# Layers 0 and 1: recurrent values, attention values and gates made by token in one 400-column product, from two weight chunks cut by input block

## The reference, cut to what matters

```
(au, av, az, bq, bk, bv, bz, cq, ck, cv, co, cz, cg) = _split_proj(xn @ w_in)
v_lat = bv.reshape(B_, S, B_KV_HEADS, HEAD_DIM)       # attention values, 2 x 64 columns
ql, kl, vl = mheads(cq), mheads(ck), mheads(cv)       # recurrent heads, 4 x 64 columns
li_f, lf_f, li_b, lf_b = gates(cg)                    # 16 gate columns
```

## Time and profile before

| | |
|---|---|
| median of 3 runs | 1133.12 us (1132.96 to 1134.46) |
| span of the profiled execution | 1130.7 us (the page gives no other time of it) |
| TensorE busy | 1100.2 us, 97% of the span |
| VectorE, ScalarE busy | 722.0 us (64%), 591.5 us (52%) |
| granted TensorE clock | 0.9 or more of full speed in all 40 slices |
| low parts of weights (L420) | 256 of 1.234 us |
| high parts of weights (L405) | 256 of 1.049 us |
| loads | 167.03 MB, mean 148 GB/s; 363 and 318 GB/s in the first two slices of 28 us |

### The profile page before, as it was taken

How to read it: one execution, slowest core, us unless ns; L and a number is a source line. 1 busy time by engine, 2 the same in 40 slices (tenths; PEclk the granted TensorE clock), 3 DMA queues, 4 the chain that set the end, 5 groups by cost and what they waited for, 6 DMA issues and landing times.

```text
span 1130.7 us, 20229 instructions
## 1 busy us (share of the span) xinstructions
PE 1100.2 (97%) x8280; PEld 969.1 (86%) x8280; DVE 722.0 (64%) x1221; ACT 591.5 (52%) x970; POOL 134.2 (12%) x160
## 2 busy tenths in 40 slices
PE   8999999999999999899999999999998999999998
PEld 6787888766777989689988999999997799999997
DVE  5546567376535667767764676766676666776674
ACT  5332666444334556757464664544474646454454
POOL 0000000054020000423232100000013321000000
PEclk9999999999999999999999999999999999999999
DMA  9822212177421333034333445455442234545551
GB/s 363 318 112 75 75 38 75 40 279 278 150 75 41 147 137 134 2 131 168 140 122 113 150 186 198 177 187 186 178 172 101 97 127 139 200 183 187 190 192 47
DMA packets 24428, 167.03 MB, mean 148 GB/s; under 512 B 2832, under 2 KB 3216, under 8 KB 4752
## 3 DMA queue, kind: packets, MB, share of 16 engines
q1 hardware_dynamic: 24336, 165.74, 39.9%
HBM read 164.68 MB, written 1.05 MB: 147 GB/s over the span
## 4 chain that ended last, share of the span: by engine, by line
PE 86%; DVE 5%; ACT 4%; issue 2%; POOL 1%; DMA 1%; SPq 0%; DVEq 0%; ACTq 0%; POOLq 0%
PE bank L426 24%; PE bank L427 23%; PE bank L428 23%; DVE wlo L420 2%; ACT whi L405 2%; PE bank L1522 2%; PE bank L1388 2%; PE bank L472 1%; DMA PROJ<-in_stream 1%; PE bank L1532 1%; PE bank L1542 1%; PE bank L1415 1%; PE bank L1406 1%; PE bank L2489 1%; PE bank L1263 1%
## 5 line engine op out<-in xcount | busy, mean ns | idle before, releaser
L426 PE MATMUL bank<-OPH,whi 128*128 128x256 f32 (+1 forms) x1716 | 524.1, 305 | 5.5 <-ACT AV L2723 2.2
L427 PE MATMUL bank<-OPL,whi 128*128 128x256 f32 (+1 forms) x1716 | 514.5, 300 | 0.0
L428 PE MATMUL bank<-OPH,wlo 128*128 128x256 f32 (+1 forms) x1716 | 514.5, 300 | 0.0
L420 DVE TENSOR_TENSOR wlo<-raw,whi 128x1024 fp32r<-128x1024 f32 x256 | 305.3, 1234 | 103.9 <-ACT whi L405 103.7
L426 PEld LDWEIGHTS bank<-OPH,whi 128*128 128x128 f32 x1716 | 327.8, 191 | 27.1 <-issue 9.8
L427 PEld LDWEIGHTS bank<-OPL,whi 128*128 128x128 f32 x1716 | 328.0, 191 | 12.1 <-issue 1.7
L428 PEld LDWEIGHTS bank<-OPH,wlo 128*128 128x128 f32 x1716 | 327.9, 191 | 11.0
L405 ACT ACTIVATE whi<-raw 128x1024 fp32r<-128x1024 f32 x256 | 255.6, 1049 | 100.7 <-PE bank L428 99.9
L426 PE MATMUL bank<-whi,OPH 128*128 128x256 f32 (+1 forms) x272 | 89.2, 328 | 0.0
L427 PE MATMUL bank<-wlo,OPH 128*128 128x256 f32 (+1 forms) x272 | 87.2, 321 | 0.0
L428 PE MATMUL bank<-whi,OPL 128*128 128x256 f32 (+1 forms) x272 | 87.1, 320 | 0.0
(11 more groups left out here) (289 smaller groups left out, 1200.5 us busy)
## 6 DMA issues: line engine op xcount, KB each, us to landing
raw<-in_stream SPq DMA_DIRECT2D x147, 1024.0 KB, 4.8
PROJ<-in_stream SPq DMA_DIRECT2D x5, 1024.0 KB, 14.9
X<-in_x_in SPq DMA_DIRECT2D x4, 512.0 KB, 6.5
C<-in_con SPq DMA_DIRECT2D x1, 1477.5 KB, 9.6
out<-PROJ SPq DMA_DIRECT2D x4, 256.0 KB, 2.1
WST<-in_w_s SPq DMA_DIRECT2D x2, 256.0 KB, 5.4
PROJ<-in_last_gain SPq DMA_DIRECT2D x1, 512.0 KB, 5.6
BS<-in_b_s SPq DMA_DIRECT2D x1, 256.0 KB, 5.9
```

Source lines behind the costliest of these rows:

```text
L420: nc.vector.tensor_tensor(c.w[1][:, part], c.raw[:, part], c.w[0][:, part].bitcast(F32), ALU.subtract).then_inc(*raises(c.lo[h]))
L426: nc.tensor.matmul(out, w[0], x[0], start=start, stop=False, skip_group_check=skip)
L427: nc.tensor.matmul(out, w[0], x[1], start=False, stop=False, skip_group_check=skip)
L428: return nc.tensor.matmul(out, w[1], x[0], start=False, stop=stop, skip_group_check=skip)
```

## The change

The attention values, recurrent values and gates of a token tile (256 + 128 + 16 = 400 columns) become one job by token, four jobs per layer; ScalarE empties each with two copies into `VA` and into a new `VG`, whose last 16 columns are the gates. The values product, the gate product and their turns go, as does the own load of the gate weights. Attention keys, these 400 columns and no more (528 in all) stand in two head chunks of 128 x 2112: the first holds input blocks 0 to 3, the second blocks 4 to 7. They come first: the first after pair 1, the second after pair 2, and the recurrent keys' chunk after all pairs. The start fills the four jobs and the keys; the two key products follow as whole jobs, `ck_0` before the gate sums and `ck_1` after. The turn of the recurrent keys moves behind `ck_1`. `rotate_keys` uses pairs of 64-column stationary slices of `ident` and `rot16` in place of `dup` and `duprot`.

```diff
-            if i == 1:
-                early = take(2)
+            if i in (1, 2):
+                early += take(1)
...
+    def heads(w):
+        at = [256 * IN_BLOCK[name] for name in ("bkv", "cv")] + [256 * IN]
+        c = np.concatenate([w[:, at[0]:at[0] + P], w[:, at[1]:at[1] + 256], w[:, at[0] + P:at[0] + 256],
+                            w[:, at[2]:at[2] + 16]], 1)
+        return c.reshape(2, 4, P, HEAD).transpose(0, 2, 1, 3).reshape(2, P, WIDE)
...
-                for j in (ck0, ck1):
+                for j in by_token:
                     first.fill_part(e, j, (0, 1))
                 pairs[2].multiply(e, 0)
-                for j in (ck0, ck1):
+                first.fill_part(e, keys, (0, 1))
+                for j in by_token[0:2]:
                     first.fill_part(e, j, (2, 3))
                 pairs[2].multiply(e, 1)
-                first.fill_part(e, keys, (0, 1))
+                for j in by_token[2:4]:
+                    first.fill_part(e, j, (2, 3))
                 pairs[2].turn(e)
+                pairs[3].multiply(e, 0)
                 first.fill_part(e, keys, (2, 3))
-                pairs[3].multiply(e, 0)
-                first.fill_part(e, values, (0, 1))
+                for j in by_token[0:2]:
+                    first.fill_part(e, j, (4, 5))
                 pairs[3].multiply(e, 1)
-                first.fill_part(e, values, (2, 3))
+                for j in by_token[2:4]:
+                    first.fill_part(e, j, (4, 5))
                 pairs[3].turn(e)
...
                 pairs[1].copy_rows(e, "act")
                 split_hi(e, 1)
                 act_operand(e, 1)
-                split_hi(e, 2)
                 pairs[2].copy_rows(e, "act")
                 act_operand(e, 2)
+                split_hi(e, 2)
...
+            heads = [j for j in jobs if j.head is not None]
+            if heads:
+                heads[-1].frees_head = True
+                heads[-1].head[0].used = ("head_half_used", heads[-1].head[0].i)
+                heads[-1].head[1].used = heads[-1].u.full
...
             def split_next(e, who, j):
+                if j.frees_head:
+                    split_ahead(e, who, j.head[1].s + 1 + SPLIT)
...
+            def evict_tokens(e, u, tt):
+                for point in due(e, ("va_ones_set",)):
+                    e.wait_ge(*point)
+                nc.scalar.activation(VA[:, tt, :, 0:HD], u.mem[:, 0:256].rearrange("p (h d) -> p h d", d=HD),
+                                     ACT.Copy).then_inc(*raises(("cv_copied", l, tt)))
+                nc.scalar.activation(VG[:, tt, :], u.mem[:, 256:BY_TOKEN], ACT.Copy).then_inc(*raises(u.read["act"]))
+
+            cv = [Job([(None, lambda m: m[:, 0:BY_TOKEN], KD,
+                        lambda k, tt=tt: (op(k, P * tt, P), head(k, P, BY_TOKEN)))], "act",
+                      lambda e, u, tt=tt: evict_tokens(e, u, tt)) for tt in range(TT)]
...
+                    def twice(out, m, kv, x):
+                        for at in (0, 64):
+                            mm = nc.tensor.matmul(out[at:at + 64, :], m[:, 64 * kv:64 * kv + 64], x, start=True, stop=True)
+                        return mm
...
-                pr.filled_together(("gates_fm", "ck_0", "ck_1", "keys"))
-                for name in ("gates_fm", "ck_0", "ck_1", "keys"):
+                names = ("cv_0", "cv_1", "cv_2", "cv_3", "keys")
+                pr.filled_together(names)
+                for name in names:
                     pr.emptied(name)
-                job("values_fm")
-                pr.turn_gates()
+                pr.give_gates()
                 rc.log_forget()
+                job("ck_0")
+                rc.cumulate()
+                hn.square("k")
+                job("ck_1")
+                rc.running_maxima()
                 rc.turn_keys()
```

More of the change, by code:

```diff
@@ L553, in start @@
             sq = [tile.take("act", ("pe",) if k == KD - 1 else ("dve",)) for k in range(KD)]
-            tot = ABANK.take("pe", ("act",))
+            spare_banks = ring_of(banks[4:7])
+            tot = spare_banks.take("pe", ("act",))
             sq[-1].freed[:] = [tot.full]
@@ L560, in start @@
             for p in pairs:
-                p.take(ABANK, "act")
+                p.take(spare_banks, "act")
             def pe(e):
                 first = s.first
-                ck0, ck1, keys, values = first.jobs[0:4]
+                by_token, keys = first.jobs[0:TT], first.jobs[TT]
                 keep_clock(e, pairs[0].row.mem, 36, pairs[0].row.empty)
@@ L984, in product @@
                         part[0].used = j.u.full
-            mine = [c for j in jobs for c, *_ in j.parts if c is not None]
+            heads = [j for j in jobs if j.head is not None]
[3 more added lines that the diff above has]
+                heads[-1].head[1].used = heads[-1].u.full
+            mine = [c for j in heads for c in j.head] + [c for j in jobs for c, *_ in j.parts if c is not None]
             first = mine[0]
@@ L1013, in fill_part @@
                     for n, (c, o, nk, pair) in enumerate(j.parts):
-                        for point in due(e, j.u.empty, [("gate_w_hi",), ("gate_w_lo",)] if c is None else c.lo[k // 4],
-                                         op_block(k)):
+                        weights = c.lo[k // 4] if j.head is None else j.head[k // 4].lo[k % 4 // 2]
+                        for point in due(e, j.u.empty, weights, op_block(k)):
                             e.wait_ge(*point)
@@ L1018, in fill_part @@
                         mm = products(o(j.u.mem), w, x, k == 0 and n == 0, k == nk - 1, skip=len(j.parts) > 1)
+                if j.frees_head and ks[-1] == 3:
+                    mm.then_inc(*raises(j.head[0].used))
                 if ks[-1] == nk - 1:
@@ L1124, in projections, with head @@
-            gates_fm = Job([(None, lambda m: m[few, :], KD,
-                             lambda k: ((GWH[:, l, k, :], GWL[:, l, k, :]), op(k, 0, T)))], "dve",
-                           lambda e, u: fill("dve", e, gt, gt.mem[few, :], u.mem[few, :], u))
+            halves = [cs["head0"], cs["head1"]]
+            for c in halves:
+                c.n = WIDE
+            def head(k, lo, n):
+                at = k % 4 * HEAD + lo
+                return tuple(w[:, at:at + n] for w in halves[k // 4].w)
@@ L1161, in projections @@
             s.keys = keys.u.freed
+            s.values = [k for j in cv for k in j.u.freed]
+            s.gates = [("gates_given", l)]
             s.q = [q[b if l == 0 else b // 2].u.freed for b in range(4)]
@@ L1174, in emptied @@
                 st.dve = lambda e: p.empty_bank(e, "dve", j)
-            def turn_values():
-                u, st = BESIDE.take("pe", ("act",)), stage(f"values{l}")
-                vt.freed[:] = [u.full]
-                def pe(e):
-                    for point in due(e, vt.full, u.empty, ("ident_loaded",)):
-                        e.wait_ge(*point)
-                    for b in range(TT):
-                        mm = nc.tensor.transpose(u.mem[:, P * b:P * (b + 1)], vt.mem[:, P * b:P * (b + 1)], ident)
-                    mm.then_inc(*raises(u.full))
-                def act(e):
-                    for point in due(e, u.full):
-                        e.wait_ge(*point)
-                    nc.scalar.activation(VB[:], u.mem[:].rearrange("p (t n) -> p t n", n=P), ACT.Copy).then_inc(
-                        *raises(u.read["act"]))
-                st.pe, st.act = pe, act
-                s.values = u.freed
@@ L1212, in dve @@
                                             GB[:, l, :].unsqueeze(1).broadcast_to([P, TT, 16]),
-                                            ALU.add).then_inc(*raises(u.read["dve"]))
-                st.pe, st.dve = pe, dve
-                s.gates = u.freed
+                                            ALU.add).then_inc(*raises(("gates_given", l)))
+                st.dve = dve
             def filled_together(names):
```

157 lines of the change are left out of this document (58 added, 99 removed).

## The result

The changed kernel took 1139.76 us (four executions, 1138.41 to 1141.73), the kernel before 1133.79: ratio 1.0054, 95% interval 1.0040 to 1.0067. In a later series the changed kernel gave 1140.44 against 1133.85, ratio 1.0053 (1.0040 to 1.0065). It is 6.0 us slower; 1133.7 was forecast, and the range ended at 1138.3. The profiled execution took 1138.78 us, its span is 1137.0, 6.3 over the one before.

What follows compares the result with a forecast made beforehand. TensorE's matmul queue, busy 97% of the span, was taken as the bound. +0.6 (layer 0), -0.9 (layer 1) and +0.85 (rotation) gave +0.55 on 1130.7; with 2.4 from span to median, 1133.7 us, range 1128 to 1138.3.

Steps and rivals of the forecast that it cites:

- Work spared: TensorE's products in each layer: 23.47 us become 96 matmuls of 400 columns at 0.180, 17.3 us; 12.3 us less in all.
- The waits: TensorE in both layers' heads and key products: new waits for operands, splits, gates and copies, 12.7 us come and 0.8 goes.
- The gates' wait of layer 1: After layer 1's key product 0, the gate sums wait for VectorE to make the gates ready: 0.9 us.
- Layer sums: Work and waits per layer, without the rotation: layer 0 ends 0.6 us later, layer 1 gains 0.9 us.
- The rotation: Keys' rotation in both layers: 64-partition halves overlap except one 512-column pass, adding 0.43 us per layer, 0.85 in all.
- the sum: Whole kernel: +0.6 - 0.9 + 0.85 = +0.55 us on a span of 1130.7.
- the two long new waits: TensorE waits 2.9 us before layer 0's blocks 4 and 5, and 3.5 us before layer 1's key product 0.
- the first rival: The clock falls behind the 2.9 and 3.5 us waits, costing up to 1.5 and 1.8 us, 1137 in all; chance 0.25.
- the 2.2 us wait of the earlier trace: TensorE's longest wait in the kernel before; its granted clock stayed at the upper level, 2.4 GHz.
- The rival's price: Matmuls behind the two long waits lose half the fall's length, taken as the wait's: up to 1.5 and 1.8 us.

Runs made afterwards that it cites:

- The three that were taken away one by one: Changed kernel with one edit each: second head chunk split earlier, 1134.61 us; layer 1's key chunk split earlier, 1136.37; layer 0's gates ahead of the keys' copy, 1136.94.
- The two sized bridges: Changed kernel with 12 and 13 unused matmuls on ones in its waits before layer 0's blocks 4 and 5 and layer 1's key product 0: 1136.47 us.
- the kernel with gates first: Changed kernel with layer 0's gate bias and forget values ahead of the keys' copy and four low halves on VectorE: 1136.94 us, ratio 1.0030.
- four bridges: Changed kernel with 12, 7, 13 and 8 unused matmuls on ones before blocks 4 and 5, blocks 6 and 7, layer 1's key product 0, at the latent: 1138.31 us.

## Why the prediction was wrong

- **Work spared: right.** 0.184 us for 400 columns against 0.180, on the line between its neighbours. The Trainium skill's rule (TensorE: Matmul & The Clock Gate, Back-to-back issue gap) gave 0.169, which the measurement doesn't bear out.
- **The waits: right in place, and five of them in size.** The three that were taken away one by one gave back their length and part of the clock. The gates' wait of layer 1 is 0.3 us at full clock, not 0.9.
- **Layer sums: nearly right.** At full clock layer 0 is 1.46 us longer from first product to scores, where +0.6 and 0.43 for the rotation were forecast, layer 1 0.43 shorter, where 0.9 less 0.43 was. That the second agrees so well is luck: 0.6 us too much for the gates' wait and 0.43 for the rotation stand against 0.4 of work (96 x 0.004) and two waits that grew by 0.2 us each.
- **The rotation: the size was off.** 2.75 us against (109.63 + 1.02) - 107.81 = 2.84 before. The halves overlap entirely; the 0.43 a layer that I added is nothing. From the last product matmul ahead of this stretch to the second one behind it both kernels take the same, 115.04 - 111.19 = 3.85 us and 110.72 - 106.87 = 3.85. The drain at a change of tiling mode that the Trainium skill states (TensorEngine Tiling (Array Packing), Key Properties) can't be judged by this comparison: the state update ahead of the rotation is 64 columns wide in both kernels, so each changes the mode twice, and the edit only moves the second change behind the rotation.
- **An unseen wait.** At 642 us TensorE waits 0.78 us for VectorE's addition to X, where the kernel before doesn't; VectorE's low part two groups earlier starts 0.35 us later after its high part than before (0.88 against 0.53). The wait is in all twelve profiles of the changed kernel and its variants and in none of the six of the kernel before and its own. Why the low part starts later, no run tells. How 0.35 us becomes a wait of 0.78, the rows show, of the changed kernel and then of the kernel before (`L870` and `L875` are the same additions of the norm's squares on GpSimd):

```profile
638.94 2.70 DVE L914 SCALAR_TENSOR_TENSOR OPL<-X,V,OPH 128x256 fp32r<-128x256 f32 x4
639.93 2.84 POOL L870 TENSOR_TENSOR TILE<-TILE 128x512 f32<-128x512 f32 x2 [20.74 <-ACT TILE L862]
```
```profile
633.89 1.67 DVE L919 SCALAR_TENSOR_TENSOR OPL<-X,V,OPH 128x256 fp32r<-128x256 f32 x4
635.25 4.58 POOL L875 TENSOR_TENSOR TILE<-TILE 128x512 f32<-128x512 f32 x3 [20.75 <-ACT TILE L867]
```

  Before, the fourth operand low part begins 0.16 us ahead of GpSimd's first instruction and takes 0.48 us; now it begins 0.20 us behind it, takes 1.51 us and ends 0.27 us after it, and the addition to X stands behind it. That one slows the other is read from this pair of profiles, not tested.
- **The step that failed is what the sum puts behind the two long new waits: nothing.** It counts 2.9 and 3.5 us as waits and no more, and leaves a fall of the clock behind them to the first rival, at a chance of 0.25. I let the granted clock of one profile speak for the 2.2 us wait of the earlier trace rows and concluded that waits up to that length are safe and 2.9 and 3.5 perhaps. In the 15 profiles that have that wait unfilled, 13 show a fall at it (3 of 5 of the kernel before and its variants, all 10 of the changed one and its); the profile before was one of the two without. The long new waits had falls in 4 of 4 profiles (3.18 us) and 3 of 4 (3.46 us). The rival's price, half of the fall's length, was right in layer 0, 1.6 us; in layer 1 it is 1.0, in part because the slower product covered the 0.3 us wait for the gates. In the profiled pair the 6.3 us are 1.26 of the start, 1.46 and 1.59 in layer 0 (work with waits, and the fall), -0.43 and 1.02 in layer 1, 0.78 at 642 us and 0.88 in the stretch with the fall at 854 us, 6.56 together; small differences elsewhere take 0.26 off.
- **The rest is chance of the start.** First products begin between 27.0 and 28.8 us in the profiles of the changed kernel and its variants, and between 27.2 and 28.7 in those of the kernel before and its own; the 1.26 us between the two profiles isn't shown to be the change's.

In sum, for medians: the clock's mean is 0.0054 lower, which is 0.0054 x 1138/(3.41/2) = 3.6 falls of 3.4 us; executions of the kernel before at a clock of 0.996 take 1135.0 us, at 0.999 1132.5, 2.5 for two falls. That would be 4.6 of 6.0 us. The two sized bridges, at the clock of the kernel before, leave 2.2 us, and so 3.8 for the clock. The part that is not clock agrees better with this second number: 1.46 - 0.43 in the layers and 0.78 at 642 us are 1.8. So the clock is 3.8 to 4.6 us of the 6.0. This division is worked out, not run as one experiment.

## What to carry to other kernels

A wait of TensorE costs more than its length where it is long: of 27 waits of 2.2 to 3.5 us behind the start in these profiles 24 had a fall of the clock, which adds 1.0 to 1.6 us unless something behind it waits anyway. Before relying on one profile's clock, compare it with the clocks of all executions: a profile above their mean hides falls. And when a product is shortened that others hid behind, move what it hid first: here the same saving lost 6 us with the splits left in line and gained 11 with the splits, the gates and the last modulation pair moved into idle stretches. What these moves alone would give the kernel before was not run; its only wait over 0.15 us between its first product and the scores of layer 0 is one of 0.77, so there is little for them to take there.

## What was not expected of the hardware

- Falls last 3.41 us or twice that (6.83), except the one that the end of the kernel cuts off. Behind longer waits they are more frequent, with no sharp border: counted behind the start in all 18 profiles, none behind the 18 waits of 1.37 or 1.38 us (but one behind 1.34, above), 1 of 18 at 1.55 to 1.66, 4 of 19 at 1.73 to 1.78, 3 of 8 at 1.96 or 1.97, 13 of 15 at 2.25, 11 of 12 at 2.29 to 3.46.
- A fall can begin inside a wait: in the profile of the kernel with gates first it runs from 364.5 to 371.3 us, where the wait before the key product ends at 365.1.
- Filling waits may move falls: with four bridges the first came at 876 us and lasted twice as long. With the wait before blocks 4 and 5 filled, the next one, of 1.97 us, had a fall in 2 of 2 profiles (60 and 57 us), and in 1 of 6 otherwise. What decides it beside the length of the wait stays open.
- Two groups of 64 output partitions cost nothing over one of 128: the rotation's sixteen instructions took 2.75 us.
